# Transposes of a hybrid decoder step in 64-row blocks, and a score bias laid into PSUM by transposes

## The chip, the cores and the metric

The kernel runs on one core of a Trainium2 chip. The metric is the device time of one execution in microseconds (us). A core has TensorE (matmuls, and the loads of their stationary operand), VectorE (DVE in the profile), ScalarE (ACT), GpSimd (POOL) and SyncE (SP), which starts transfers. TensorE writes only to PSUM, which has eight banks of 128 partitions by 512 floats; VectorE and ScalarE copy from there to SBUF.

## The reference, cut to what matters

One inference step of four layers for a prompt of 256 tokens and a sample group of 8 sequences with 4 new tokens each, 288 columns in all. The width is 1024. Each layer is a half feed-forward block, a mixer, and another half feed-forward block. Layers 0 and 3 mix by RWKV-7, layer 1 by differential attention with a relative-position bias, layer 2 by gated DeltaNet. All is float32. What the change touches is this:

```
# RWKV-7, samples: the old state S0 (8 sequences, 16 heads, 64 x 64, [value, key]) enters the recurrence
S = S * w_t + sa * b_t + v_t * k_t
# differential attention, 8 heads of width 128 = [k1 | k2]
s1 = q1 @ k1.T * scale + bias;   s2 = q2 @ k2.T * scale + bias      # bias: by distance of query and key
o  = (softmax(s1) - lam * softmax(s2)) @ v
# prompt: k, v of its own 256 tokens; samples: 256 past rows in two pages of 128 rows of the
# paged caches cache_attn_k, cache_attn_v, and 4 own tokens each; k and v of all new tokens are outputs too
```

## The kernel before

Each engine has its own instruction list, written out by hand, and counts semaphores up and down the line (`after(x)` waits for the next count of x). Activations are kept transposed, channels on the partitions, tokens along the row: `W(i)[:, c, :]` is chunk c of 128 channels. Dense layers are three matmuls a chunk (lines 1018 to 1020), for each weight piece that ScalarE and VectorE have split in a high and a low part; this is most of the kernel. Weights come through a ring of slots that SP fills ahead.

**RWKV layers.** The prompt runs in chunks of 64 tokens. Each chunk inverts a triangular matrix in a ladder of steps (`chunk_inverse`): matmuls at line 1434, a copy, matmuls at line 1461, a copy. During the ladder of chunk 0 TensorE also turns the old sample states from [value, key] to [key, value]: `sample_transposes(b, old)`, line 1538, makes eight transposes of 128 x 128 for two sequences and fills banks 4 and 5. Batch 0 stands ahead of the ladder; batches 1 to 3 come behind steps 1 to 3 (`behind`). ScalarE copies bank 4 (line 2451), VectorE bank 5 (line 3063). Later `sample_state` (line 1577) turns the new states back: it is written with blocks of 64 rows and 128 columns already, which alternate between the two halves of the partitions (`HALVES`) and between two banks.

**Attention layer, pages.** Q is projected first. Then `four_sequences(0)` handles the past keys of sequences 0 to 3: eight units u, each of four heads of one sequence. `page_transposes(u)` (line 1632) is eight 128 x 128 transposes into two banks; ScalarE copies one of them (line 2574), VectorE the other (line 3248) to `pageT[u % 2]`; `page_scores(u)` (line 1642) multiplies. TensorE's order is T(0), T(1), S(0), T(2), S(1), ... T(7), S(6), S(7). In this first phase ScalarE also makes two weight splits (`in_w_high`) and VectorE two (`in_w_low`, line 3221) between its copies. Then K and V are projected, and `four_sequences(8)` does the same for sequences 4 to 7, without splits between. GpSimd loads pages with `load_pages`, and the bias table `hankel` (line 3798) once V is projected.

**Tokens.** K and V are transposed for three token tiles (128, 128, 32) at line 1675, eight transposes of each; ScalarE copies K (line 2602), VectorE V (line 3305). The second tile waits for `s_biased`, the end of VectorE's sums and maxima of the sample scores. The V copy of the third tile stands on VectorE behind the sample softmax (lines 3311 to 3317), and `scores(1)` waits for it.

**Prompt scores.** 16 jobs n: head n // 2, query block n % 2, which sees 128 (even n) or 256 (odd n) keys. `scores(n)` lays the bias into two banks with a matmul by the identity (line 1685, two halves `sub` of the head), then adds Q K (line 1688). A float32 matmul is two instructions in the profile, a transpose is one. VectorE takes maxima (line 3326), ScalarE the exponentials, VectorE the difference (lines 3332 to 3336); TensorE transposes it (line 1704) and multiplies by V (line 1713). TensorE's order is scores(n), transposes(n - 2), values(n - 3) and, for n = 8 to 11 and 14 to 17, the page values (line 1724). VectorE's order is maxima(n), difference(n - 1), copy of the output of n - 3 (line 3341). `hankel[:, hd, :]` holds f(partition + column).

## Time and profile before

| what | value |
|---|---|
| median of 3 runs | 2789.84 us (2788.41 to 2793.72) |
| profiled execution | 2786.35 us |
| span of the profiled execution | 2784.7 us |
| TensorE matmul busy | 2722.6 us (98%) |
| VectorE busy | 1670.1 us (60%) |
| ScalarE busy | 1238.1 us (44%) |
| GpSimd busy | 286.3 us (10%) |
| HBM traffic | 144 GB/s mean |

Times within the trace count from the start of the span. The RWKV ladders with the state transposes run at about 362 to 380 and 2401 to 2418 us, the attention's page phases at 981.7 to 994.9 and 1047.2 to 1060.5, its tokens to 1068 and its prompt scores to 1113. Matmul durations overlap: the mean duration of one instruction is much longer than the distance to the next.

### The profile page before, as it was taken

Reading aid. Unit: us, or ns where it says so; the run is one execution under the profiler, and the core shown is the slowest. Engines: PE = TensorE matmul, PEld = TensorE weight load, DVE = VectorE, ACT = ScalarE, POOL = GpSimd, SP = SyncE. Lnnn points to the kernel's source line nnn. Section 1 sums busy time; section 2 is a strip of 40 time slices with the busy share of each in tenths; the row PEclk is TensorE's granted clock in tenths of the full one; section 3 lists DMA queues with packets and bytes.
Section 4 is the critical chain, followed back from the end, with each engine's and each line's share of the span. In section 5 each row is a group of like instructions: output and inputs, shape, how many; then the busy total and the mean of one; then the engine's idle time right before and its main releaser. Section 6 shows DMA issues by size and latency. Waiting matters only on the chain.

```text
span 2784.7 us, 60598 instructions
## 1 busy us (share of the span) xinstructions
PE 2722.6 (98%) x26597; PEld 2576.4 (93%) x26597; DVE 1670.1 (60%) x2529; ACT 1238.1 (44%) x1988; POOL 286.3 (10%) x343
## 2 busy tenths in 40 slices
PE   9999999999999999999999998999999999999999
PEld 8997988999999986999999997789999979788999
DVE  5646866665565546665565594546556558866653
ACT  5435644543443334544443474234344356445443
POOL 2001023000000102000000121410000010122001
PEclk9999999999999999999999999999999999999999
DMA  9444401553654655444653443254465353306442
GB/s 284 132 143 140 139 33 35 186 169 125 202 162 134 242 186 201 136 157 133 193 172 125 144 163 120 70 178 145 145 188 165 127 170 122 63 4 186 151 134 80
DMA packets 351611, 402.47 MB, mean 145 GB/s; under 512 B 31290, under 2 KB 306127, under 8 KB 350989
## 3 DMA queue, kind: packets, MB, share of 16 engines
q1 hardware_dynamic: 340448, 361.73, 40.5%
q0 software_dynamic: 10976, 38.07, 4.4%
q8 instruction: 139, 2.28, 0.3%
q14 instruction: 48, 0.39, 0.0%
HBM read 385.19 MB, written 14.57 MB: 144 GB/s over the span
## 4 chain that ended last, share of the span: by engine, by line
PE 89%; DVE 6%; ACT 2%; issue 1%; DMA 1%; SPq 0%; POOL 0%; DVEq 0%; ACTq 0%; POOLq 0%
PE banks L1018 24%; PE banks L1020 24%; PE banks L1019 24%; PE banks L1461 1%; PE banks L1434 1%; PE banks L1161 1%; PE banks L1008 1%; PE banks L1632 1%; PE banks L1585 1%; PE banks L1950 1%; PE banks L1069 1%; DVE ring_lo L2947 1%; PE banks L1409 0%; DVE h L2862 0%; PE banks L1479 0%
## 5 line engine op out<-in xcount | busy, mean ns | idle before, releaser
L2877 DVE TENSOR_TENSOR w_lo<-ring,w_hi 128x2048 fp32r<-128x2048 f32 (+1 forms) x303 | 609.0, 2010 | 410.7 <-ACT w_hi L2326 410.7
L1018 PE MATMUL banks<-h_hi,w_hi 128*128 128x288 f32 x2816 | 836.9, 297 | 2.3 <-DVE x L3204 1.4
L1019 PE MATMUL banks<-h_hi,w_lo 128*128 128x288 f32 x2816 | 831.4, 295 | 0.0
L1020 PE MATMUL banks<-h_lo,w_hi 128*128 128x288 f32 x2816 | 828.5, 294 | 0.0
L2326 ACT CAST w_hi<-ring 128x2048 fp32r<-128x2048 f32 (+1 forms) x303 | 509.5, 1682 | 574.6 <-PE banks L1020 543.7
L1018 PEld LDWEIGHTS banks<-h_hi,w_hi 128*128 128x128 f32 x2816 | 528.3, 188 | 4.7 <-DVE h_lo L2869 1.9
L1020 PEld LDWEIGHTS banks<-h_lo,w_hi 128*128 128x128 f32 x2816 | 531.0, 189 | 0.0
L1019 PEld LDWEIGHTS banks<-h_hi,w_lo 128*128 128x128 f32 x2816 | 529.4, 188 | 0.4
L1018 PE MATMUL banks<-hid_hi,w_hi 128*128 128x288 f32 x1408 | 416.2, 296 | 0.0
L1019 PE MATMUL banks<-hid_hi,w_lo 128*128 128x288 f32 x1408 | 415.4, 295 | 0.0
L1020 PE MATMUL banks<-hid_lo,w_hi 128*128 128x288 f32 x1408 | 414.4, 294 | 0.0
L1020 PEld LDWEIGHTS banks<-hid_lo,w_hi 128*128 128x128 f32 x1408 | 265.1, 188 | 0.0
L1019 PEld LDWEIGHTS banks<-hid_hi,w_lo 128*128 128x128 f32 x1408 | 264.3, 188 | 0.0
L1018 PEld LDWEIGHTS banks<-hid_hi,w_hi 128*128 128x128 f32 x1408 | 263.9, 187 | 0.0
L2825 ACT CAST hid_hi<-work 128x288 fp32r<-128x288 f32 x176 | 76.2, 433 | 397.8 <-DVE work L3622 397.8
L3678 POOL TENSOR_TENSOR h<-h 128x288 f32<-128x288 f32 x65 | 78.9, 1215 | 1510.2 <-ACT h L2255 903.7
L3614 DVE TENSOR_TENSOR work<-banks,rinv 128x288 f32<-128x288 f32 x176 | 80.5, 458 | 174.1 <-PE banks L1020 174.1
L3624 DVE TENSOR_TENSOR hid_lo<-work,hid_hi 128x288 fp32r<-128x288 f32 x176 | 80.7, 459 | 87.8 <-ACT hid_hi L2825 87.8
L1019 PE MATMUL banks<-h_hi,ring_lo 128*128 128x288 f32 x448 | 132.6, 296 | 0.0
L1019 PEld LDWEIGHTS banks<-h_hi,ring_lo 128*128 128x128 f32 x448 | 84.9, 190 | 0.1
L3637 DVE SCALAR_TENSOR_TENSOR x<-banks,x 128x288 f32<-128x288 f32 x64 | 29.3, 457 | 85.8 <-PE banks L1020 85.8
L3622 DVE TENSOR_TENSOR work<-work 128x288 f32<-128x288 f32 x176 | 79.5, 451 | 1.8 <-ACT work L2823 1.8
(607 smaller groups left out, 4228.6 us busy)
## 6 DMA issues: line engine op xcount, KB each, us to landing
ring<-in_ffn_w_gate SPq DMA_DIRECT2D x87, 1024.0 KB, 5.5
ring<-in_ffn_w_up SPq DMA_DIRECT2D x87, 1024.0 KB, 8.0
ring<-in_ffn_w_down SPq DMA_DIRECT2D x64, 768.0 KB, 4.6
ring<-in_ffn_w_down SPq DMA_DIRECT2D x64, 640.0 KB, 5.8
ring<-in_rwkv_w_rkv SPq DMA_DIRECT2D x24, 1024.0 KB, 6.4
ring<-in_gdn_w_in SPq DMA_DIRECT2D x16, 1024.0 KB, 7.4
ring<-in_attn_w_qkv SPq DMA_DIRECT2D x12, 1024.0 KB, 7.4
ring<-in_rwkv_w_o SPq DMA_DIRECT2D x8, 1024.0 KB, 6.2
```

Of the source, the lines that this page charges most:

```text
L1008: last = nc.tensor.matmul(bank[at][:, 0:NT], ones[:, :], h[:, c, :], start=(c == 5), stop=(c == 7))
L1018: nc.tensor.matmul(out, w_hi_k, x_hi_k, start=start, stop=False)
L1019: nc.tensor.matmul(out, w_lo_k, x_hi_k, start=False, stop=False)
L1020: return nc.tensor.matmul(out, w_hi_k, x_lo_k, start=False, stop=stop)
L2326: nc.scalar.copy(w_hi[e][:, 0:k, :], raw).then_inc(w_hi_ready, 1)
L2825: nc.scalar.copy(hid_hi[:, 2 * u + e, :], prod[:, e, :]).then_inc(act_hi_ready, 1)
L2877: nc.vector.tensor_tensor(w_lo[e][:, 0:k, :], raw, w_hi[e][:, 0:k, :], ALU.subtract).then_inc(w_lo_ready, 1)
L3614: nc.vector.tensor_tensor(silu[:, e, :], bank[2 * e][:, 0:NT], rinv[:, :], ALU.mult)
L3622: nc.vector.tensor_tensor(prod[:, e, :], silu[:, e, :], prod[:, e, :], ALU.mult).then_inc(prod_ready, 1)
L3624: nc.vector.tensor_tensor(hid_lo[:, f, :], prod[:, e, :], hid_hi[:, f, :], ALU.subtract).then_inc(act_lo_ready, 1)
L3637: nc.vector.scalar_tensor_tensor(x[:, c, :], bank[4 + c % 4][:, 0:NT], 0.5, x[:, c, :], ALU.mult, ALU.add).then_inc(x_updated, 1)
L3678: nc.gpsimd.tensor_tensor(h[:, c, :], h[:, c, :], h[:, other, :], ALU.add).then_inc(presummed, 1)
```

## The change

Pages, the K and V of the tokens, and the old sample states are transposed in blocks of 64 rows: for each block of 128 x 128, one transpose of rows 0 to 63 and one of rows 64 to 127, each with a 64 x 64 identity as the moving operand. The two alternate, and the halves go to two different banks. So a bank now holds one half of all eight blocks where it held both halves of four; ScalarE and VectorE copy the same banks as before, with the same number of elements, to destinations of 64 floats out of every 128. The bias of the prompt scores is laid by transposes of 128 x 128 blocks of `hankel`, where a matmul by the identity stood: one for an even job's half, two for an odd one's; a block of f(partition + column) is its own transpose. Nothing else moves, and no wait is added or removed.

```diff
--- before.py
+++ after.py
@@ -1532,12 +1532,13 @@
 
             def sample_transposes(b, old):
 
-                for i in range(2):
-                    for q in range(4):
-                        hp = 4 * i + q
-                        last = nc.tensor.transpose(bank[4 + i][:, 128 * q:128 * q + 128],
-                                                   old[:, 4 * b + hp // 2, 128 * (hp % 2):128 * (hp % 2) + 128], ident)
-                    last.then_inc(seq_t_raw, 1)
+                for hp in range(CH):
+                    for i, r in enumerate(HALVES):
+                        last = nc.tensor.matmul(bank[4 + i][:, 64 * hp:64 * hp + 64],
+                                                old[r, 4 * b + hp // 2, 128 * (hp % 2):128 * (hp % 2) + 128], ident64[r],
+                                                is_transpose=True, start=True, stop=True)
+                        if hp == CH - 1:
+                            last.then_inc(seq_t_raw, 1)
 
             def states_read(i, turned, apart):
 
@@ -1629,8 +1630,10 @@
                     for q in range(4):
                         for g in range(2):
                             c = 128 * (4 * a + q)
-                            last = nc.tensor.transpose(bank[2 * (u % 2) + q // 2][:, 256 * (q % 2) + 128 * g:256 * (q % 2) + 128 * g + 128],
-                                                       pages[b_ % 4][:, g, c:c + 128], ident)
+                            for i, r in enumerate(HALVES):
+                                last = nc.tensor.matmul(bank[2 * (u % 2) + i][:, 64 * (2 * q + g):64 * (2 * q + g) + 64],
+                                                        pages[b_ % 4][r, g, c:c + 128], ident64[r],
+                                                        is_transpose=True, start=True, stop=True)
                     last.then_inc(pageT_raw, 1)
 
                 def page_scores(u):
@@ -1672,8 +1675,10 @@
                         if i == 2:
                             after(ready)
                         for c in range(CH):
-                            last = nc.tensor.transpose(bank[TOK_BANK[i] + 2 * w + c // 4][0:tn, 128 * (c % 4):128 * (c % 4) + 128],
-                                                       W(src)[:, c, t0:t0 + tn], ident)
+                            for e, r in enumerate(HALVES):
+                                last = nc.tensor.matmul(bank[TOK_BANK[i] + 2 * w + e][0:tn, 64 * c:64 * c + 64],
+                                                        W(src)[r, c, t0:t0 + tn], ident64[r],
+                                                        is_transpose=True, start=True, stop=True)
                         last.then_inc(raw, 1)
                 after(hankel_in, 16)
                 jobs = [(hd, qt) for hd in range(AH) for qt in range(2)]
@@ -1682,11 +1687,13 @@
                     hd, qt = jobs[n]
                     nk, back = 128 * (qt + 1), 128 - 128 * qt
                     for sub in range(2):
-                        nc.tensor.matmul(bank[2 * (n % 2) + sub][:, 0:nk], ident, hankel[:, hd, back:back + nk], start=True, stop=False)
+                        for k in range(qt + 1):
+                            nc.tensor.matmul(bank[2 * (n % 2) + sub][:, 128 * k:128 * k + 128], hankel[:, hd, back + 128 * k:back + 128 * k + 128], ident,
+                                             is_transpose=True, start=(k == 0), stop=False, skip_group_check=True)
                     for sub in range(2):
                         r = slice(64 * sub, 64 * sub + 64)
                         last = nc.tensor.matmul(bank[2 * (n % 2) + sub][:, 0:nk], W(Q_)[r, hd, 128 * qt:128 * qt + 128], W(1)[r, hd, 0:nk],
-                                                start=False, stop=True)
+                                                start=False, stop=True, skip_group_check=True)
                     last.then_inc(score_raw, 1)
 
                 def sample_probs():
@@ -2448,7 +2455,7 @@
 
                 def turned_states(i):
                     after(seq_t_raw, 2)
-                    nc.scalar.copy(turned[i][:, 0:4].rearrange("p c b n -> p (c b n)"), bank[4][:, :]).then_inc(seq_t_ready_act, 1)
+                    nc.scalar.copy(turned[i][:, :, 0, :], bank[4][:, :].rearrange("p (c n) -> p c n", n=64)).then_inc(seq_t_ready_act, 1)
 
                 def sample_copy(raw, dst, at, ready):
                     after(raw)
@@ -2571,7 +2578,7 @@
                 def page_copies(u0):
                     for u in range(u0, u0 + 8):
                         after(pageT_raw)
-                        nc.scalar.copy(pageT[u % 2][:, 0:512], bank[2 * (u % 2)][:, :]).then_inc(pageT_ready_act, 1)
+                        nc.scalar.copy(pageT[u % 2].rearrange("p (c e n) -> p c e n", e=2, n=64)[:, :, 0, :], bank[2 * (u % 2)][:, :].rearrange("p (c n) -> p c n", n=64)).then_inc(pageT_ready_act, 1)
                         if u in (1, 3):
                             in_w_high(8 + u // 2)
 
@@ -2599,7 +2606,7 @@
                 for i, (t0, tn) in enumerate(TOK_TILES):
                     after(ktok_raw)
                     for e in range(2):
-                        last = nc.scalar.copy(akey[0:tn, i, 512 * e:512 * e + 512], bank[TOK_BANK[i] + e][0:tn, :])
+                        last = nc.scalar.copy(akey[0:tn, i, :].rearrange("p (c e n) -> p c e n", e=2, n=64)[:, :, e, :], bank[TOK_BANK[i] + e][0:tn, :].rearrange("p (c n) -> p c n", n=64))
                     last.then_inc(ktok_ready, 1)
                     if i == 0:
                         after(s_biased)
@@ -3060,7 +3067,7 @@
 
                 def turned_states(i):
                     after(seq_t_raw, 2)
-                    V.tensor_copy(turned[i][:, 4:8].rearrange("p c b n -> p (c b n)"), bank[5][:, :]).then_inc(seq_t_ready_dve, 1)
+                    V.tensor_copy(turned[i][:, :, 1, :], bank[5][:, :].rearrange("p (c n) -> p c n", n=64)).then_inc(seq_t_ready_dve, 1)
 
                 def decayed(i):
                     return TT(turned[i], turned[i], PLpair[:, :, :, i:i + 1].broadcast_to([128, CH, 2, 64]), ALU.mult)
@@ -3245,7 +3252,7 @@
                 def page_copies(u0):
                     for u in range(u0, u0 + 8):
                         after(pageT_raw)
-                        V.tensor_copy(pageT[u % 2][:, 512:1024], bank[2 * (u % 2) + 1][:, :]).then_inc(pageT_ready_dve, 1)
+                        V.tensor_copy(pageT[u % 2].rearrange("p (c e n) -> p c e n", e=2, n=64)[:, :, 1, :], bank[2 * (u % 2) + 1][:, :].rearrange("p (c n) -> p c n", n=64)).then_inc(pageT_ready_dve, 1)
                         if u in (2, 4):
                             in_w_low(s, 7 + u // 2)
 
@@ -3302,7 +3309,7 @@
                     tn = TOK_TILES[i][1]
                     after(vtok_raw)
                     for e in range(2):
-                        last = V.tensor_copy(aval[0:tn, i, 512 * e:512 * e + 512], bank[TOK_BANK[i] + 2 + e][0:tn, :])
+                        last = V.tensor_copy(aval[0:tn, i, :].rearrange("p (c e n) -> p c e n", e=2, n=64)[:, :, e, :], bank[TOK_BANK[i] + 2 + e][0:tn, :].rearrange("p (c n) -> p c n", n=64))
                     last.then_inc(vtok_ready, 1)
 
                 token_values(0)
```

## Rows read from the trace of the kernel before

**Rows 1.** The page, parts 1 and 2: busy time; granted clock in 40 slices.
```profile
PE 2722.6 (98%) x26597; PEld 2576.4 (93%) x26597; DVE 1670.1 (60%) x2529; ACT 1238.1 (44%) x1988; POOL 286.3 (10%) x343
PEclk9999999999999999999999999999999999999999
```
**Rows 2.** Views by line: duration of one instruction (ns min/median/max), whole and half transposes.
```profile
L1538 PE MATMUL banks<-consts,ring x64: 272/273/329, 362.4 to 2415.4; 128*128 128x128 f32 x64
...
L1577 PE MATMUL banks<-consts,ring x128: 221/222/273, 451.2 to 2510.1; 64*128 64x64 f32 x128
```
**Rows 3.** Timeline of PE (start, length, line, count): a batch of each kind.
```profile
362.40 1.04 PE L1538 MATMUL banks<-consts,ring 128*128 128x128 f32 x8
...
461.07 0.71 PE L1577 MATMUL banks<-consts,ring 64*128 64x64 f32 x16
```
**Rows 4.** Chain in order of time (start, length, what), RWKV layer 0.
```profile
367.01 1.02 PE banks L1538 x8
...
464.58 0.64 PE banks L1577 x16
```
**Rows 5.** Chain in order of time, first page phase.
```profile
981.74 1.75 PE banks L1632 x16
...
984.22 1.02 PE banks L1632 x8
985.25 0.59 PE banks L1642 x16
...
993.37 0.70 DVE work L3248
...
994.20 0.67 PE banks L1642 x16
```
**Rows 6.** Chain in order of time, start of the second page phase.
```profile
1047.17 1.90 PE banks L1632 x16
```
**Rows 7.** Timeline of DVE, first page phase: a copy, a split, a copy.
```profile
985.28 0.69 DVE L3248 COPY work<-banks 128x512 f32<-128x512 f32 x1 [1.07 <-PE banks L1632]
985.89 1.22 DVE L3221 TENSOR_TENSOR ring_lo<-ring,in_w_hi 128x1024 fp32r<-128x1024 f32 x1
987.02 0.68 DVE L3248 COPY work<-banks 128x512 f32<-128x512 f32 x1
```
**Rows 8.** Group by line and shape, DVE: the copies of `new_states`, which have a strided destination.
```profile
L3071 DVE COPY ring<-banks 128x512 f32<-128x512 f32 x8 | 5.5, 691 | 16.9 <-PE banks L1585 16.9
```
**Rows 9.** Chain in order of time, the second token tile.
```profile
1063.47 1.98 PE banks L1675 x16
```
**Rows 10.** Timeline, DVE: V copies of the second tile, idle time before them in brackets.
```profile
1065.47 1.29 DVE L3305 COPY work<-banks 128x512 f32<-128x512 f32 x2 [0.86 <-PE banks L1675]
```
**Rows 11.** Chain in order of time, bias matmuls of jobs 1, 5, 9 and 10.
```profile
1070.02 1.13 PE banks L1685 x4
...
1078.28 0.87 PE banks L1685 x4
...
1087.92 1.06 PE banks L1685 x4
...
1091.22 0.64 PE banks L1685 x4
```
**Rows 12.** Timeline of DVE in the score loop: maxima of an odd job.
```profile
1079.82 0.69 DVE L3326 TENSOR_REDUCE acol<-banks 128x2 f32<-128x512 f32 x1 [0.61 <-PE banks L1688]
```
**Rows 13.** Windows: busy us (instructions) of each engine, granted clock, DMA share, GB/s.
```profile
10.00:15.00 5.00, 3.10 (x11) 1.68 (x11) 3.38 (x7) 2.76 (x6) 0.00 (x0) 0.50 1.20 295
...
1060.00:1068.00 8.00, 6.32 (x67) 5.33 (x52) 6.52 (x14) 5.16 (x14) 3.26 (x7) 1.00 1.03 409
1068.00:1113.00 45.00, 41.89 (x478) 29.81 (x476) 30.18 (x100) 19.28 (x83) 8.63 (x19) 1.00 0.38 140
```
**Rows 14.** Chain in order of time, dense matmuls ahead of and behind a rise of the clock.
```profile
16.43 0.24 PE banks L1018
...
19.10 0.13 PE banks L1018
```

## The prediction, made before the changed kernel was run

> **What bounds the kernel now.** I read the page first: TensorE is busy for 2722.6 of 2784.7 us, and its granted clock stays in the top tenth in every slice [rows 1]. So what TensorE no longer does comes off the end, unless another engine was about to be late. Then I read the views by line and the chain in order of time at the five places that the change touches, to see for each whether the edited instructions lie on the chain and who is next. All of them together last some 15 us in the RWKV ladders, 27 us in the page phases and 53 us from the tokens to the end of the prompt scores; the rest of the span is untouched.
>
> **What a block costs in either form.** A batch of eight whole transposes takes 1.04 us from its first start to its last end, and one of them 0.273 [rows 2, 3], so the distance between two is (1.04 - 0.273) / 7 = 0.110 us. The half form is in the kernel already, with the same shapes (64 rows by 128 columns stationary, 64 columns moving, alternating halves and banks): sixteen take 0.71 us, one 0.222 [rows 2, 3], so the distance is (0.71 - 0.222) / 15 = 0.0325 us, and two halves cost 0.065 where a whole cost 0.110. In line with other work the batch of eight adds 1.02 us to the chain, and the sixteen halves 0.64 [rows 4]. Both figures contain a step from one shape to another: 1.02 - 7 x 0.110 = 0.25, and 0.64 - 15 x 0.0325 = 0.15 us. So a batch of eight blocks that lies on the chain gets 0.38 us shorter, the value that I take. If the step vanished between the page products (64 rows) and half blocks (64 rows), it would be 0.53; if the halves did not overlap at all, it would be a loss (third rival).
>
> The trace thus shows a step of about 0.15 to 0.25 us at each change of shape. The Trainium skill, TensorEngine Tiling (Array Packing), Tiling Modes, says that a change of the tiling mode, not of the tile alone, drains the engine. With modes counted by rows alone, pages would lose the step altogether and the sum would be some 3 us better (22 batches by 0.15, an estimate); with modes counted by rows and columns it stays, since the page products are 32 columns wide. My sum keeps it.
>
> **Old sample states.** Four batches in each of two layers. Batch 0 stands ahead of a wait of TensorE for ScalarE, so its gain is hidden. Batches 1 to 3 are links of the chain, 1.02 us each [rows 4], and all that follows them on VectorE and ScalarE is released by them, so it comes earlier with them. 2 x 3 x 0.38 = **2.3 us**.
>
> **Pages, second phase.** The first two batches took 1.90 us and the first products 0.67 behind them [rows 5, 6], 2.57 in all. Now the first batch ends after about 0.65, and the products wait for its copy: 0.04 (hand-over, estimated from the 0.13 that the return takes) + 0.69 (copy) [rows 7] + 0.13 (from the end of a copy to the products) + 0.67 [rows 5] make 2.18; gain 0.38 in round numbers. The other six batches go from 1.02 to 0.64: 2.28. Between the end of a batch and the products that need its copy lie the products before and the next batch, 0.59 + 0.64 = 1.23 us, and the copy wants 0.04 + 0.69 + 0.13 = 0.86: it still hides. The last products wait for the last copy as before [rows 5]. **2.66 us**.
>
> **Pages, first phase.** The same, but the start took 1.75 + 0.07 + 0.67 = 2.49 [rows 5], which gives 0.30, and VectorE makes a weight split of 1.13 us (start to start, [rows 7]) twice between copies. A unit of TensorE's work shrinks from 1.61 to 1.23 us, and a split and a copy (0.61 start to start) together take 1.74: written out unit by unit, the products of unit 3 are 0.2 us late for the copy, those behind the second split not. 0.30 + 2.28 - 0.2 = **2.4 us**. Keys of sequences 4 to 7 are loaded in the first phase for the second, so no transfer is drawn into it.
>
> **The copies** keep bank, size and order. Their destinations become strided by 64 floats in 128. A strided copy of the same size takes 691 ns [rows 8], the contiguous ones 0.69 us [rows 7]; I take nothing for it.
>
> **Tokens.** The first tile's 16 transposes run beside VectorE's sums and maxima, so nothing. The second tile's 16 are on the chain, 1.98 us [rows 9]: from an idle engine 32 halves want 31 x 0.0325 + 0.222 = 1.23. VectorE was idle for 0.86 us ahead of its V copy [rows 10] and is free in time. The third tile's V copy and job 1's scores follow on VectorE. 0.75, of which I take **0.7 us**. The first scores also wait for the bias table's transfer, which starts with the second page phase; in the trace no wait of TensorE ends with it, but DMA is saturated in this stretch, share 1.03 [rows 13], and the scores come some 3 us sooner after its issue. I put that at 0 to 1 us and take 0.
>
> **The bias.** A job's bias was four instructions, 0.87 us on the chain for an odd job behind 128-row work, 1.06 behind the page values and 1.13 from idle; an even job 0.64 behind page values [rows 11]. Now it is four transposes (odd) or two (even): 4 x 0.110 = 0.44, and 3 x 0.110 + 0.25 = 0.58 behind page values, 3 x 0.110 + 0.273 = 0.60 from idle, 0.110 + 0.25 = 0.36 for an even job there. On the chain are the eight odd jobs: job 1 gives 0.53, jobs 3, 5, 7, 13 give 0.43, jobs 9, 11, 15 give 0.48; of the even ones only 10 and 12, 0.28 each. The other even jobs run while TensorE waits for VectorE's difference anyway, and only lengthen that wait. Sum 0.53 + 4 x 0.43 + 3 x 0.48 + 2 x 0.28 = 4.25. What is late next is VectorE: ahead of an odd job's maxima it had 0.61 us idle [rows 12], now 0.61 - 0.43 = 0.18, so it is not yet the bound. I take **4.2 us**. Below zero the term can't well go: fewer passes of the same columns through the same banks.
>
> **Sum.** 2.3 + 2.4 + 2.7 + 0.7 + 4.2 = 12.3 us, 0.44%. The profiled execution of 2786.35 us would be near 2774.1 (span 2772.4). It lay 3.5 us below the median of the runs shown, 2789.84, on which the prediction stands: **2777.6 us**.
>
> **The rivals.**
> 1. *The score loop does not pay.* VectorE's rounds have only 0.18 us left by my count; if its loop closes, or the bias still waits on something else, the 4.2 us go. For it: VectorE is busy 30.2 of 45 us there [rows 13] and strung into the chain. Against it: its idle times. 8.1 us gained, 2781.7.
> 2. *The copies take the page phases.* Were the strided copies to take over 1.05 us, products would wait; at 1.6 us both phases stay at their old 1.61 us a unit. For it: no copy in the trace turns this exact layout. Against it: the strided copy's time [rows 8]. 7.2 us gained, 2782.6.
> 3. *Slower: half blocks do not overlap.* With load and stream of a half in line (0.110 is about 0.055 of load for 128 columns and 0.055 of stream for 128; a half would be 0.055 + 0.028), a pair costs 0.165, 0.055 more than a whole. 6 state batches, 16 page batches and 2 token batches are 192 blocks: 10.6 us lost, less the bias' 4.2: 2796.2. It decides from a pair of 0.110 + 4.2 / 192 = 0.132 us up. Against it stands the measured 0.065 of the same shapes.
> 4. *Slower: the clock.* In the token stretch nearly all of TensorE's work was transposes and it was idle for 1.7 of 8 us, and yet the granted clock was 1.00 (2.4 GHz) [rows 13]. At 0.50 (1.2 GHz), granted in 10 to 15 us behind idle stretches [rows 13], a dense matmul took 0.24 us a step, at full clock 0.13 [rows 14]. If the score loop fell to that, its 41.9 busy us less 4.2 would grow by 0.8 of themselves, 30 us; less the 12.3, 2807.6. The Trainium skill, TensorE: Matmul & The Clock Gate, Part 4, says that transposes do not count as busy for the clock in the way that matmuls do; by that rule, more of them in place of matmuls would bring this about. The trace disagrees with it in the token stretch.
> 5. *It is absorbed.* Later waits for splits or transfers eat it: 0 to 5 us gained. Against it: the chain behind the attention and the ladders is TensorE's.
>
> **How the numbers follow.** My forecast 0.75, rival 1 0.10, rival 2 0.05, rival 5 0.06, rival 3 0.03, rival 4 0.01. Upwards the steps that might vanish give 3.3 us more gain, and the runs shown spread by some 3 us about their median: low end 2771.5. To the other side rivals 1 and 2 with the same spread reach 2784.5. Faster by over 0.2% (5.6 us; about what a measurement of this kernel can tell from no change) holds most of my forecast and of rivals 1 and 2: 0.84. Same 0.12, slower 0.04.
>
> **What would show it.** Sixteen halves (lines 1538, 1632 of before) add about 0.64 us to the chain; a page unit is near 1.23; copies stay at 0.69 and 0.59; odd bias steps are near 0.44 to 0.60; VectorE's idle ahead of odd maxima shrinks to some 0.2, and TensorE's wait for the difference of even jobs grows by 0.3. Wrong would be: a copy above 1.05 us, a batch above 1.02, a clock below 1.00 in the attention, or a new wait behind 1113 us.

## The result, and the profile of the changed kernel

The changed kernel takes 2775.29 us (median of 3 runs, 2771.17 to 2775.44) where the kernel before takes 2789.84. The ratio is 0.9948, 95% interval 0.9934 to 0.9962: faster by 0.5%, inside the forecast range and 2.3 us below its centre. The profiled execution has a span of 2773.6 us against 2784.7, 11.1 us less; the sum said 12.3. That the total fits does not mean that every term did: several unforeseen effects of 1 to 2 us cancelled, so the parts are read one by one.

The lines of the change moved by a few: 1538 of before is now 1537 (state transposes), 1632 is 1634 (page transposes), 1642 is 1645 (page products), 3248 is 3255 (VectorE's page copy), 1675 is 1679 (tokens), 1685 is 1691 (bias), 1688 is 1695 (Q K), 3326 is 3333 (maxima), 3335 is 3342 (first step of the difference).

**The batches.** The chain in order of time (start, length, what), first in an RWKV ladder, then in the first page phase. They answer to [rows 4] and [rows 5].

```profile
365.72 0.65 PE banks L1537 x16
...
977.83 0.41 ACT work L2601
978.24 0.02 issue
978.26 0.31 DVE work L3287 x2
978.57 0.02 issue
978.59 0.70 DVE work L3255
979.29 0.14 issue
979.43 0.67 PE banks L1645 x16
980.10 0.64 PE banks L1634 x16
980.74 0.59 PE banks L1645 x16
```

A batch of eight blocks adds 0.64 to 0.65 us, as forecast (1.02 before), and a page unit is 0.64 + 0.59 = 1.23 us. The start of the phase differs from the forecast: the first VectorE copy (978.59) waits for ScalarE's copy of Q's last sum and for two products of VectorE, not for the batch, so part of the first batch's gain is hidden (0.18 us gained where the forecast had 0.30).

**The second page phase** in the same view, which answers to [rows 6]:

```profile
1041.00 0.66 PE banks L1634 x16
...
1048.14 0.65 PE banks L1634 x16
1048.79 0.33 PE banks L1645
1049.12 0.85 issue
1049.97 0.66 PE banks L1645 x15
```

The pace is the forecast one up to 1049. Then TensorE stands still for 0.85 us in the middle of a group of products, with nothing shown that it waits for, and the group starts over: its pieces take 0.33 + 0.66 us where the other groups take 0.59. The loss is 0.85 + 0.40 = 1.25 us. Nothing in the trace of before has this.

**The copies** with their strided destination (by line: ns of one, min/median/max) are what the contiguous ones were [rows 7]:

```profile
L3255 DVE COPY work<-banks x16: 681/692/692, 978.6 to 1051.3; 128x512 f32<-128x512 f32 x16
```

**The score loop.** The chain through jobs 1, 3, 5, 7, 9 and 10 (bias at L1691, Q K at L1695), answering to [rows 11]:

```profile
1061.75 0.86 PE banks L1691 x4
1062.61 1.18 PE banks L1695 x4
...
1066.06 0.85 PE banks L1691 x4
1066.92 1.18 PE banks L1695 x4
...
1072.06 0.44 PE banks L1691 x4
1072.50 0.66 PE banks L1695 x4
...
1075.95 0.44 PE banks L1691 x4
...
1080.86 0.59 PE banks L1691 x4
...
1083.68 0.37 PE banks L1691 x2
```

From 1072 on the odd jobs' bias takes 0.44 behind 128-row work and 0.59 behind the page values, the even job's 0.37: the forecast 0.44, 0.58 and 0.36. The first two odd jobs show 0.86, and their Q K 1.18 instead of 0.66, all about twice as long. The windows (busy us and count of each engine, granted clock, DMA share, GB/s) tell why:

```profile
1060.00:1062.00 2.00, 1.88 (x15) 1.36 (x16) 2.00 (x5) 0.21 (x1) 0.92 (x3) 1.00 1.03 406
1062.00:1068.00 6.00, 5.52 (x23) 2.94 (x21) 3.07 (x10) 3.31 (x15) 0.47 (x1) 0.50 0.81 328
...
1075.00:1113.00 38.00, 35.81 (x440) 23.77 (x441) 22.92 (x76) 20.01 (x71) 5.01 (x12) 1.00 0.33 113
```

Six microseconds of the loop ran at a granted clock of 0.50, 1.2 GHz. In before the same stretch has 1.00 [rows 13]. What went ahead of it stands on the timeline of PE, and from 1068 on of POOL and DVE (in brackets: idle time before, and who ended it); first the place in before, then in the changed kernel:

```profile
1067.67 0.57 PE L1685 MATMUL banks<-work,consts 128*128 128x128 f32 x3 [0.49 <-ACT work L2602]
```

```profile
1060.12 0.41 PE L1691 MATMUL banks<-consts,work 128*128 128x128 f32 x2 [2.09 <-ACT work L2609]
...
1068.74 1.82 POOL L3818 MEMSET work<- 128x2076 f32 x1 [6.28 <-DMA attn_v_s<-work]
...
1068.92 0.21 DVE L3340 TENSOR_SCALAR acol<-acol 128x1 f32<-128x1 f32 x1
1069.17 1.48 DVE L3342 TENSOR_SCALAR work<-work,acol 128x128 f32<-128x128 f32 x1
...
1073.18 0.69 DVE L3333 TENSOR_REDUCE acol<-banks 128x2 f32<-128x512 f32 x1 [0.18 <-PE banks L1695]
```

Three things. TensorE is idle for 2.09 us until ScalarE has copied K (before: 0.49 us), and 2 us later the clock falls. It had been idle for 1.93 us ahead of the second token tile as well; in the 6.1 us ahead of the first scores it was busy for 2.11 us, in before for 4.42 (the first row is before's, the second the changed kernel's):

```profile
1061.57:1067.67 6.10, 4.42 (x39) 3.74 (x38) 5.13 (x10) 5.03 (x14) 2.01 (x5) 1.00 1.03 408
...
1054.00:1060.10 6.10, 2.11 (x64) 1.96 (x65) 5.84 (x12) 4.67 (x14) 2.01 (x5) 1.00 1.03 408
```

The first step of VectorE's difference takes 1.48 us instead of 0.30, until GpSimd's MEMSET ends (1068.74 + 1.82 = 1070.56); in before the same MEMSET ran from 1074.96 on and met such a step only at its very end (0.33 us for 0.29). And the row of L3333 answers to [rows 12]: VectorE's idle time ahead of the maxima is 0.18 us, the 0.61 - 0.43 of the forecast.

**Where 11.1 us came from.** I paired every VectorE instruction of the two traces in order and took the start in before less the start in after; where this difference grows, time is gained. Its steps, in order of time:

| stretch | us gained | forecast |
|---|---|---|
| start-up, first 20 us (arrival of x) | +1.35 | - |
| ladder of layer 0 | +1.14 | 1.15 |
| clock fall near 493 us: 6.8 us long in before, 3.4 in after | +1.5 | - |
| first page phase | +2.2 | 2.4 |
| second page phase: 2.65, less 1.25 at the stand-still | +1.4 | 2.7 |
| tokens | +0.75 | 0.7 |
| score loop: 4.2 of the bias, less 1.9 (clock) and 1.2 (MEMSET) | +1.1 | 4.2 |
| clock fall at 1113 us, only in after | -1.5 | - |
| dense layers between | +1.1 | 0 |
| ladder of layer 3 | +1.14 | 1.15 |
| clock fall near 2530 us: 6.8 us in before, 3.4 in after | +0.9 | - |

The first and third row, the dense layers and the last row (+4.85 together) stand in work that the change doesn't touch. Falls of the clock come there in every trace, the bias-only and whole-transpose kernels included: near 493 and near 2530 us in all of them, at other places in some, 3.4 to 17.1 us long. Over the 48 runs of before beside the experiments (whole transposes apart), the time goes with the execution's mean granted clock, 1.3 us for each 0.001 of it, which explains 60% of the variance between runs. The attention in turn lost 1.25 + 1.9 + 1.2 + 1.5 = 5.85 us against the sum, and 0.2 in the first phase: 12.3 + 4.85 - 6.05 = 11.1. The experiments had to find which of these losses belong to the change.

### The profile page after: what moved, and what is told of

It reads as the page before. It is cut to its first block, busy times and chain, and to the rows that moved or that the text cites. A ratio compares the mean times of both kernels' runs of the same rounds, so it can differ in the third digit from the quotient of the medians.

```text
span 2773.6 us, 61046 instructions
## 1 busy us (share of the span) xinstructions
PE 2711.3 (98%) x26821; PEld 2565.9 (93%) x26821; DVE 1671.0 (60%) x2529; ACT 1238.3 (45%) x1988; POOL 286.2 (10%) x343
## 4 chain that ended last, share of the span: by engine, by line
PE 89%; DVE 6%; ACT 3%; issue 1%; DMA 1%; SPq 0%; POOL 0%; DVEq 0%; ACTq 0%; POOLq 0%
PE banks L1018 24%; PE banks L1020 24%; PE banks L1019 24%; PE banks L1461 1%; PE banks L1434 1%; PE banks L1161 1%; PE banks L1008 1%; PE banks L1586 1%; PE banks L1069 1%; PE banks L1957 1%; DVE ring_lo L2954 1%; PE banks L1409 0%; DVE h L2869 0%; PE banks L1479 0%; PE banks L2099 0%
```

## The experiments

**1. The bias alone, and the blocks alone.** Rival 1 (the loop does not pay) against the forecast. The first kernel is before with only the new bias, the second the changed kernel with the old one:

```
-                        nc.tensor.matmul(bank[2 * (n % 2) + sub][:, 0:nk], ident, hankel[:, hd, back:back + nk], start=True, stop=False)
+                        for k in range(qt + 1):
+                            nc.tensor.matmul(bank[2 * (n % 2) + sub][:, 128 * k:128 * k + 128], hankel[:, hd, back + 128 * k:back + 128 * k + 128], ident,
+                                             is_transpose=True, start=(k == 0), stop=False, skip_group_check=True)
```

> The kernel before with the bias laid by transposes alone; all other transposes are whole ones. My theory: odd jobs' bias falls from 0.87 to 0.44 us on the chain, 4.2 us in all; because nothing ahead of the score loop is shorter, GpSimd's clearing of 1.82 us begins at about 1075 as before, while the loop is half a microsecond further, and may hold a VectorE step for up to 1 us. So 3.2 to 4.2 us faster than before. Rival (VectorE closes the loop): 0 to 1 us.

> The changed kernel with the bias laid by identity matmuls as before. My theory: the blocks of 64 rows give 2.3 us in the two ladders, 2.2 and 2.6 in the page phases, 0.7 in the tokens, 7.8 us in all, less up to 1.7 where the clock falls behind the idle stretch ahead of the first scores. 6 to 8 us faster than before. Rival (the blocks give no more than the copies let through): under 4 us.

Measured: bias alone 2784.99 us against 2788.14, ratio 0.9987 [0.9978, 0.9996], 3.2 us less (the interval is 1 to 6 us); blocks alone 2780.74, ratio 0.9974 [0.9965, 0.9983], 7.4 us less (5 to 10). Together 10.6 us. Both forecast halves (4.2 and 8.1) lie within 1 us of that. In the bias-only trace the score loop is 3.65 us shorter, and the missing half microsecond is a row there too, on DVE's timeline, with POOL's:

```profile
1077.48 0.84 DVE L3337 TENSOR_SCALAR work<-work,acol 128x128 f32<-128x128 f32 x1
...
1076.42 1.82 POOL L3813 MEMSET work<- 128x2076 f32 x1 [3.80 <-DMA attn_v_s<-work]
```

The step is held until 1078.3, where the MEMSET ends. In the blocks-only trace the clock falls at 1061.1 us for 3.4, and the stand-still is there with 1.14 us: so neither comes from the new bias.

**2. One half, then the other.** The same half blocks in the same banks, but all of the upper row half first, for states, pages and tokens; so consecutive ones now also write the same bank. This measures what prediction and third rival differed on, the overlap. The edit for the states (the others are likewise):

```
-                for hp in range(CH):
-                    for i, r in enumerate(HALVES):
+                for i, r in enumerate(HALVES):
+                    for hp in range(CH):
```

> The changed kernel with all upper halves of a batch first and all lower halves behind them, the same instructions and banks. My theory: what makes a half cost 0.0325 us is that its load goes beside the stream of the other rows; in line it costs about 0.055 of load and 0.028 of stream, so a batch of sixteen takes about 1.3 to 1.5 us on the chain where it takes 0.65, and 24 such batches on the chain cost 15 to 20 us more than the changed kernel: near 2792 us. Rival (halves are cheap because they move only 64 columns, whatever the order): a batch stays at 0.65 to 0.9 and the time within 6 us of the changed kernel's.

Measured: 2783.22 us, ratio 0.9984 [0.9975, 0.9993]: 4.9 us ahead of before on the same chip, where the changed kernel is ahead by 11 to 12 (part 5), so 6 to 7 us are lost. On its chain, a page batch and a state batch:

```profile
985.49 0.95 PE banks L1634 x16
...
368.45 0.95 PE banks L1537 x16
```

A batch gets 0.30 us longer, over the 24 batches on the path 7.2 us, which fits. That is (0.95 - 0.15) / 15 = 0.053 us for each half, but this mean mixes two things. The start times of the single instructions in the batch at 368.45 show the eight upper halves 0.062 to 0.064 us apart (after a first distance of 0.112), and the eight lower ones likewise; but the first lower half starts 0.007 us behind the fifth upper one, and three lower ones have started when the eighth upper one does. TensorE thus lets a half go ahead of earlier ones of the other row half, and even this order overlaps in part. In the changed kernel two of a pair start 0.003 to 0.009 us apart, and the pairs 0.062. So halves with no overlap at all would cost 0.062 each and a pair 0.124 (an estimate from these distances): more than one whole at 0.110, though not the 0.165 of the third rival, which my expectation of 1.3 to 1.5 us took over. Rival 3's mechanism exists, then, at a smaller price; without the overlap the blocks would be a small loss and not a gain.

**3. Is it the bank?** The changed blocks alternate both row halves and banks. Here before keeps its whole transposes, which only change banks from one to the next (the states' edit is shown, the pages' is likewise).

```
-                for i in range(2):
-                    for q in range(4):
+                for q in range(4):
+                    for i in range(2):
```

> The kernel before with whole transposes of 128 x 128, but consecutive ones of a batch of pages or states into different banks, as the halves of the changed kernel are. It tells the row halves apart from the bank each. Theory: the gain is that of the row halves; a batch of eight stays at 1.02 us on the chain. Rival (whole transposes into one bank hold each other up): a batch falls below 0.9 us.

```profile
366.95 1.02 PE banks L1538 x8
```

Still 1.02 us, for states and pages, and the total 2793.47 beside 2794.2 for before on that chip (one run each). Changing the bank does nothing for whole transposes, so the gain needs the row halves. Whether halves need two banks as well to overlap is open: experiment 2 changed order and bank sequence together, though there, too, the halves that overlapped lay in different banks.

**4. The idle time and the clock.** Theory: the 2.09 us of idle TensorE ahead of `scores(0)` bring the fall at 1062. It can be filled with dummy matmuls, after the V copy of the second tile and ahead of the bias table's wait:

```
                         last.then_inc(raw, 1)
+                after(vtok_ready, keep=False)
+                keep_clock(6, 2)
                 after(hankel_in, 16)
```

> The changed kernel with two dense matmuls into a free bank (0.85 us each) between the last token transpose and the first scores, where TensorE is idle for 2.1 us. My theory: the idle stretch lets the granted clock fall to 0.50 for 6.8 us from about 1062 on; with it filled the clock stays at 1.00 and jobs 1 to 3 take their full-clock times: up to 1.9 us faster than the changed kernel. Rival (the fall is a matter of the moment and not of the idle stretch): the clock falls as often, and the time is the same or 0.1 us longer.

Measured: 2774.5 us, ratio 0.9952 [0.9938, 0.9965]. The window 1062 to 1068 has the clock at 1.00, and the score loop is 2.0 us shorter than in the changed kernel's first trace, though it met the MEMSET at a worse point. The total cannot be told from the changed kernel's:

```profile
1062.00:1068.00 6.00, 4.84 (x36) 3.14 (x36) 4.65 (x16) 3.92 (x17) 0.51 (x1) 1.00 0.86 350
...
1069.49 1.68 DVE L3344 TENSOR_SCALAR work<-work,acol 128x256 f32<-128x256 f32 x1
```

The count over all traces, those of the next parts included: with the idle time left (2.09 us; in the third trace of the changed kernel 1.62), four fell at 1061 to 1062 (the changed kernel three times, blocks alone) and two did not (MEMSET in quarters, weight load held), one of them with the same 2.12 us of work in the 6.1 us before. Of the three that fill them and leave the transfers of the value pages as they are, none fell there. With one half behind the other TensorE was idle for 1.53 us ahead of the second tile's transposes (before: 1.19) and for 0.38 ahead of the first scores; the clock fell at 1064.4, 0.6 us behind the first. So the idle time seems to make a fall likely here and doesn't decide it; four of six against none of three doesn't prove it either.

**5. The changed kernel again, twice, and each suspect alone.** The first is unchanged, to see what comes again.

> The changed kernel itself, once more, beside the next ones. Both theories: 0.994 to 0.996 of the kernel before. Its trace tells whether three things come again: the clock falling to 0.50 about 1.5 us behind the start of the first scores, VectorE's step of 1.49 us under GpSimd's clearing, and a pause of TensorE of 0.85 to 1.15 us inside a page product of the second phase. If they belong to the change they are all there; if they were moments of one execution, they are gone.

Everything came again: 2777.23 us (ratio 0.9961 [0.9948, 0.9975]), the clock at 0.50 from 1061.6 for 13.7 us, a step of 1.18 us, a stand-still of 0.87. With the longer fall the score loop as a whole gained nothing here: it came out 0.3 us longer than in before, by the same pairing of VectorE's instructions.

```profile
1062.00:1068.00 6.00, 5.52 (x23) 3.10 (x21) 3.08 (x10) 3.23 (x15) 0.40 (x1) 0.50 0.79 322
...
1069.33 1.18 DVE L3342 TENSOR_SCALAR work<-work,acol 128x128 f32<-128x128 f32 x1
```

Then the MEMSET in four pieces, so that VectorE can get in between:

```
-                nc.gpsimd.memset(diff_apart, 0.0).then_inc(apart_zeroed, 1)
+                for c0 in range(0, APART + 2048, 519):
+                    last = nc.gpsimd.memset(diff_apart[:, c0:c0 + 519], 0.0)
+                last.then_inc(apart_zeroed, 1)
```

> The changed kernel with GpSimd's one clearing of 2076 columns (1.82 us) in four of 519. Theory: VectorE's scaling of the probabilities from SBUF to SBUF cannot run while a GpSimd clearing does, and waits for its end; with quarters of about 0.46 us it waits for one of them at most, so the long step falls from 1.3 to 1.7 us to under 0.8, and the kernel gains 0.5 to 1.2 us. Rival (the two are slow for another reason, as the transfers at that time): the step stays over 1.2 us.

```profile
1071.08 1.14 POOL L3819 MEMSET work<- 128x519 f32 x2 [6.15 <-DMA attn_v_s<-work]
...
1071.35 0.40 DVE L3342 TENSOR_SCALAR work<-work,acol 128x256 f32<-128x256 f32 x1
```

The longest such step is now 0.40 us (0.35 undisturbed), and the loop gains 4.12 us against before, the forecast 4.2. But in this trace the clock did not fall at 1062 either, though the idle time was there, so the 4.12 us are not the MEMSET's doing alone; the total, 2776.47 (ratio 0.9957 [0.9943, 0.997]), cannot be told from the changed kernel beside it.

The third suspect is the stand-still. On the instruction queue a packet of 16 KB started at 1047.33 and took 1.16 us, while the data queues had the DMA engines at a share over 0.9. In all nine traces with a stand-still TensorE stops at the same instruction and goes on 1.2 to 1.5 us behind that packet's end. Theory: TensorE had used up its fetched instructions. The faster second phase spends them sooner: a batch and its products have 32 where they had 24, in 1.23 us where they took 1.61, and the packets come 7.1 and 6.1 us apart (1047.33, 1054.38, 1060.49) where before has 14.1 (1039.89, 1054.03). First the next weight transfer is held on SP until all 16 page batches are issued:

```
+                        if s and stages[s - 1][0] == "attn" and j == 1:
+                            sp.wait_ge(pageT_raw, 16)
```

> The changed kernel with one weight load of 2 MB, which SP starts at 1040 us with the second page phase, held back until the last page batch is transposed. Theory: the pause inside the page product is TensorE waiting for its next 16 KB of instructions, whose transfer began at 1047.3 behind the weights; without the weights the pause shrinks to under 0.3 us or goes, 0.8 to 1.1 us gained, and nothing is late for the weights, which are used after 1100. Rival (the pause is not the transfers'): it stays at 0.85 to 1.15 us and the time is the same.

2778.29 us, ratio 0.9963 [0.9951, 0.9975]. The stand-still goes from 0.87 to 0.59 us, a part of what I expected:

```profile
1050.33 0.66 PE L1647 MATMUL banks<-work 64*32 64x256 f32 x15 [0.59 <-issue]
```

The value pages (GpSimd's queue) were still moving. So in a later kernel, with the other edits in it, they are held as well:

```
-                    pool.wait_ge(pageT_raw, 2 * (b_ + 4) + 2)
+                    pool.wait_ge(pageT_raw, 16)
```

> The kernel with all three mends, and the loads of the first four value pages held back too until the last page batch is transposed, so that at the time of the pause (1049 us) hardly any data moves. Theory: the pause inside the page product, 0.87 us in the changed kernel and 0.45 to 0.59 with the weights held back, is the fetch of instructions behind data; it goes to under 0.15 us. Rival (what is left is the latency of the fetch itself, as TensorE uses up 16 KB of instructions faster than in the kernel before): it stays at about 0.45. Time: 0 to 0.5 us less than with the three mends, unless the value pages are late.

```profile
1049.30 0.82 PE L1647 MATMUL banks<-work 64*32 64x256 f32 x16
...
1079.29 1.60 PE L1735 MATMUL banks<-work 128*32 128x128 f32 x32 [2.00 <-POOL work L3832]
```

With both quiet the gap is gone (sixteen products in one group), though the group still takes 0.75 us on the chain where the others take 0.59, so 0.16 is left of what the theory wants under 0.15. The packet itself was hardly faster: 1.12 us with the DMA engines at a share of 0.07, and in the changed kernel's trace the packets of this size take 1.10 us in the median when hardly any data moves. What changed is its start, 2.3 us ahead of the group of products here, 0.9 to 1.5 in the traces with a stand-still. So the data seem to delay the fetch and not to lengthen it; what holds up its start is not shown. The price is the second row: the page values now wait 2.00 us in the loop, as the pages come late; the clock also fell at 1055.8, 1079.7 and 1113.8. The total is 2778.85 us (0.9962 [0.9948, 0.9976]), so this is evidence and no improvement.

**6. A better version.** Idle time filled, MEMSET in quarters, weight transfer held:

> The changed kernel with the idle stretch ahead of the first scores filled by two dense matmuls, the clearing in quarters and the weight load held back. Theory: the three gains add, up to 1.9 + 1.0 + 0.9 us: near 2772 where the changed kernel has 2775 to 2776. Rival (each only gives way to the next wait): within 1 us of the changed kernel.

> The kernel with all three mends once more, beside the changed kernel. Theory: 0.9985 of the changed kernel (4 us less), and no fall of the clock between 1055 and 1075 us. Rival: within 1 us of it.

> The changed kernel as it is, to compare with the two others on one chip. 0.9955 of the kernel before, as twice already. Whether its clock falls to 0.50 at 1062 us is open by my theory, which makes it likely (idle for 2.09 us) but not certain, since it fell in the profiles of three of five kernels with this idle stretch.

All three together took 2773.08 us (ratio 0.9947 [0.9934, 0.9961]) and, a second time, 2775.39 (0.9948 [0.9935, 0.9962]); the changed kernel beside them 2777.23 and 2775.23 (0.9958 [0.9943, 0.9973]). In the first one's trace:

```profile
1062.00:1068.00 6.00, 4.49 (x31) 2.69 (x32) 5.07 (x18) 4.32 (x20) 0.01 (x1) 1.00 1.04 404
...
1070.76 0.34 DVE L3346 TENSOR_SCALAR work<-work,acol 128x128 f32<-128x128 f32 x1
```

Clock 1.00 from there to 1109, step 0.34 us, stand-still 0.45 (0.57 in the second one's), span 2769.7 us. Over both chips the ten runs have a mean of 2774.2 us and the eleven of the changed kernel beside them 2777.3: 3.2 us less, with a 95% interval of about 1 to 5. The pairs of medians differ by 4.2 and by nothing, so it is the fastest kernel here, but by little. The third trace of the changed kernel again had the clock fall (1061.7, 13.7 us), a step of 1.02 us and a stand-still of 0.85, and its score loop came out 0.1 us longer than in before.

## Why the prediction was right, and where it was not

1. **What a block costs: right.** 0.64 to 0.65 us a batch, with the step between shapes as large as in before, also between page products and half blocks. The pitch of 0.0325 us came from the halves of the returning states, the same shapes in the same kernel; that was the row that decided.
2. **States: right,** 1.14 us in each layer, 2.28 for 2.3.
3. **Pages, first phase: right but for 0.2 us** (2.2 for 2.4). The missed link is the start, 0.18 us for 0.30: VectorE's first copy stands behind two small products that wait for ScalarE. The late copy of unit 3, forecast at 0.2 us, was 0.21: 0.13 of waiting and 0.08 of longer products behind it.
4. **Pages, second phase: the pace right, the total not.** 1.4 us for 2.66. The forecast had no term for the fetch of instructions: a third more of them in a quarter less time, under saturated transfers. The stand-still (0.85) and the group of products that starts over behind it (0.40) cost the 1.25 us.
5. **Copies and tokens: right in the size** (692 ns; 0.75 us for 0.7). The 0.75 us are gained on VectorE, whose V copies job 1 waits for. The first scores themselves start no earlier, 4.25 us behind VectorE's maxima in both kernels, because ScalarE's exponentials and K copies hold them; the forecast had looked at VectorE alone. The bias table landed at 1052.2, in good time.
6. **The bias: right in its instructions, wrong in what hid beside it.** The 4.2 us are there in the trace with the MEMSET in quarters (4.12 us) and with all three edits (4.07); VectorE's idle time was 0.18 us, so its loop did not close and rival 1 falls. But in the changed kernel 1.9 + 1.2 = 3.1 of them were lost to a slower clock and to the MEMSET, and in its second and third trace, with clock falls of 13.7 us, some 4.4: all of it.
7. **Rival 3 fell, but more narrowly than stated:** with no overlap a pair would cost 0.124 us by the start times of experiment 2, below the break-even of 0.132. The 192 blocks would then have lost 192 x 0.014 = 2.7 us, and the whole change would still have been ahead by 1.5 (estimates). The price of 0.165 came from splitting the 0.110 into 0.055 of load and 0.055 of stream and keeping the whole load for a half; a half in line measures 0.062.
8. **Rival 4 came in small,** for a reason that I had not priced. The token transposes got shorter, but ScalarE's exponentials and K copies did not, so the difference turned up as TensorE's idle time, 0.49 us to 2.09, and in four of six traces the clock fell behind it, to 1.2 GHz. The fall of 6.8 us cost about 1.9 us, those of 13.7 us about 3.6 each. In the loop itself, with all its new transposes, the clock of the changed kernel was 1.00 from 1075 to 1113. The Trainium skill, TensorE: Matmul & The Clock Gate, Part 4, has transposes not count as busy in the same way as matmuls; here both the idle time and the transposes just ahead of it stood before the falls, and filling with matmuls would mend either, so the runs don't separate them. Of the eleven kernels and repeats with a bias of transposes, nine had no fall between 1076 and 1109. The two that had one, of 3.4 us (one half behind the other, at 1078.0; transfers held, at 1079.7), had it within 0.4 us of an idle stretch of 1.38 and 2.00 us; the three with the old bias had none. So the new bias does not by itself bring a fall, and whether it makes one likelier is open.
9. **Why the total fits all the same.** The losses of 6.05 us that the sum lacked were mostly met by 4.85 us at start-up, in the dense layers and in clock falls elsewhere. That is luck within the range, not accuracy. The comparisons with more runs, 0.9961 and 0.9958 beside 0.9948, put the change between 11 and 12 us, each with an interval of some 4 us to either side.
10. **Open: the fall at 1113.** Behind the score loop the granted clock fell for 3.4 us, at 1109.2 to 1115.7 us, in seven of eleven traces with the new blocks, and in none of the three without (before, the bias alone, whole transposes). In all seven it fell 9.2 to 9.9 us behind the loop's last instruction, amid the same work that before has there at full clock. That may be the change's, by the other timing with which the attention now ends, or not; no run was made for it, and its 1.5 us count as a loss above. I had named a clock below 1.00 in the attention as a sign that the prediction was wrong; it came, and the sum had no term for it.

## What to carry to other kernels

Float32 transposes of 128 rows are worth writing as 64-row blocks that alternate row halves, 0.38 us off a batch of eight; the order is what pays, since the same blocks one half after the other save only 0.07. When a stretch gets faster, ask what now stands idle and what now falls together: here the freed time became idle time ahead of a fall of the clock, a GpSimd clearing moved onto a VectorE step, and instructions seem to have come late. A total that fits the forecast is no proof of its terms; take the difference of the two traces stretch by stretch.

## What the runs showed of the hardware that I had not expected

- **GpSimd's clearing blocks some VectorE instructions entirely.** A MEMSET of 128 x 2076 floats (1.82 us) held a TENSOR_SCALAR from SBUF to SBUF of 128 or 256 columns until its own end: 1.48, 1.18, 1.02, 0.84, 0.62, 1.31, 1.68 and 0.45 us in eight traces (the changed kernel three times, bias alone, blocks alone, one half behind the other, idle time filled, weight load held), undisturbed 0.29 to 0.35. A TENSOR_SCALAR of one column (L3340, 0.21 us), the maxima read from PSUM (0.69 us), the step with two inputs from SBUF (0.48) and the copy from PSUM (0.28) ran beside it at their usual length. In quarters of 519 columns the worst is 0.40, and a quarter that begins during such a step takes 0.67 or 0.68 us where the others take 0.53: the one that starts second waits. The Trainium skill, SBUF — State Buffer, section SBUF: two separate sides, describes the port pair of VectorE and GpSimd as an exclusive lock for a whole instruction, against VectorE instructions that use two ports; the traces agree with that for the wide steps, in both directions.
- **A half transpose overlaps with one in the other row half** (two start 0.003 to 0.009 us apart, a pair every 0.062), not with one in its own (0.062 from start to start), and TensorE starts it ahead of earlier ones of the other half (three lower halves before the eighth upper one). The halves that overlapped always lay in different banks; a change of bank is worth nothing to whole ones (1.02 us either way).
- **TensorE seems to outrun its instructions.** With the data queues at work, it stood for 0.80 to 1.14 us (six traces) in a stretch of short matmuls and went on 1.2 to 1.5 us behind the end of a 16 KB packet of the instruction queue; it stood for 0.45 to 0.59 us (three traces) with one of the two data queues quiet, and not at all with both (one trace). The packet takes about 1.1 us with and without other traffic.
- **The clock fell behind a gap of 2.1 us** (1.6 in one of them) in four of six traces, to 1.2 GHz for 3.4 to 13.7 us, and not in the other two.
